# Attention inside one decoder step: the next head's projections placed between softmax steps, rope on VectorE, and the two softmax maps combined without dividing the first by its sum

## What is computed

```python
kv = rmsnorm(h, ln_kv) @ w_kv                      # K and V of all heads
k = rope(rmsnorm(k, k_norm), pos)                  # 2 maps of 64 channels each, 16 of 64 channels rotate
q = rope(rmsnorm((x @ w_q), q_norm), pos)
s = where(k_pos <= q_pos, q k^T / 8, min)          # for both maps m = 0, 1
p = softmax(s)
a = p[map 0] - lam * p[map 1]
o = a @ v                                          # sample tokens also over 256 cached positions
o = rmsnorm(o, subln) * (1 - lam_init)             # over the 128 value channels of a head
y = o @ w_out
```

## Time and profile before

| | us |
|---|---|
| Time, median of 3 runs | 3677.07 (3669.15 to 3680.99) |
| The profiled execution, its own time | 3693.18 |
| Its span, first to last instruction | 3691.4 |
| PE busy in it | 3396.5 (92%) |
| Attention, within the span | 1997 to 2801 |

### The profile page before, as it was taken

How to read it: one execution, slowest core, us unless ns; L and a number is a source line. 1 busy time by engine, 2 the same in 40 slices (tenths; PEclk the granted TensorE clock), 3 DMA queues, 4 the chain that set the end, 5 groups by cost and what they waited for, 6 DMA issues and landing times. The chain is left out here.

```text
span 3691.4 us, 60669 instructions
## 1 busy us (share of the span) xinstructions
PE 3396.5 (92%) x24063; PEld 3222.7 (87%) x24063; DVE 1512.6 (41%) x2316; ACT 1071.6 (29%) x1895; POOL 704.1 (19%) x453
## 2 busy tenths in 40 slices
PE   5898889988979999999999888888999999999998
PEld 5888878887869999999998777777878999999998
DVE  2554555455537222222234444444446422222223
ACT  2333343333321311111113344443343211111111
POOL 1212221222012311111113111111111321111110
PEclk7999999999969999999999899999999999999999
DMA  2010110011001111111111111111110111111111
GB/s 89 20 29 25 30 31 25 25 30 31 25 19 40 47 45 43 46 42 46 46 46 58 53 47 53 45 46 52 53 51 26 46 46 46 41 46 47 40 46 66
DMA packets 254695, 155.84 MB, mean 42 GB/s; under 512 B 9520, under 2 KB 251714, under 8 KB 254402
## 3 DMA queue, kind: packets, MB, share of 16 engines
q1 hardware_dynamic: 254426, 151.91, 14.1%
HBM read 133.46 MB, written 18.42 MB: 41 GB/s over the span
## 5 line engine op out<-in xcount | busy, mean ns | idle before, releaser
L212 PE MATMUL ps<-x_hi,w_hi 128*128 128x364 f32 x2808 | 667.2, 346 | 12.5 <-DVE w_lo L202 4.5
L212 PE MATMUL ps<-x_lo,w_hi 128*128 128x364 f32 x2808 | 621.8, 330 | 4.8 <-issue 4.8
L212 PE MATMUL ps<-x_hi,w_lo 128*128 128x364 f32 x2808 | 623.1, 330 | 0.0
L212 PEld LDWEIGHTS ps<-x_hi,w_hi 128*128 128x128 f32 x2808 | 486.4, 190 | 46.0 <-issue 11.5
L212 PEld LDWEIGHTS ps<-x_hi,w_lo 128*128 128x128 f32 x2808 | 491.0, 189 | 4.3 <-issue 4.3
L212 PEld LDWEIGHTS ps<-x_lo,w_hi 128*128 128x128 f32 x2808 | 490.2, 189 | 1.1 <-issue 1.1
L202 DVE TENSOR_TENSOR w_lo<-w_raw,w_hi 128x1024 fp32r<-128x1024 f32 x200 | 287.2, 1436 | 468.6 <-ACT w_hi L198 468.5
L198 ACT ACTIVATE w_hi<-w_raw 128x1024 fp32r<-128x1024 f32 x200 | 211.7, 1058 | 811.6 <-PE ps L212 594.1
L192 POOL TENSOR_TENSOR w_raw<-w_raw,params 128x1024 f32<-128x1024 f32 x120 | 234.0, 1950 | 928.8 <-DMA w_raw<-in_w_in_a 448.2
L1620 DVE TENSOR_TENSOR acc<-ps,acc 128x1092 f32<-128x1092 f32 x128 | 165.6, 1294 | 434.2 <-PE ps L212 434.2
L212 PE MATMUL ps<-hidden_hi,w_lo 128*128 128x364 f32 x1536 | 338.3, 328 | 0.0
(11 more groups left out here) (334 smaller groups left out, 4809.2 us busy)
## 6 DMA issues: line engine op xcount, KB each, us to landing
w_raw<-in_w_up SPq DMA_DIRECT2D x64, 512.0 KB, 3.9
w_raw<-in_w_down SPq DMA_DIRECT2D x64, 512.0 KB, 3.4
w_raw<-in_w_in_a SPq DMA_DIRECT2D x32, 512.0 KB, 4.2
w_raw<-in_w_kv SPq DMA_DIRECT2D x16, 512.0 KB, 4.0
cache_pages<-in_cache_k SPq DMA_DIRECT2D x128, 64.0 KB, 1.9
cache_pages<-in_cache_v SPq DMA_DIRECT2D x128, 64.0 KB, 1.9
x_in<-in_x_prompt SPq DMA_DIRECT2D x8, 512.0 KB, 4.2
state_sample<-in_state_delta SPq DMA_DIRECT2D x8, 512.0 KB, 4.0
```

The costliest lines, as they stand in the source:

```text
L212: mm = nc.tensor.matmul(PS[:, bank + g, 0:GRP], wt, x[:, k, g * GRP:(g + 1) * GRP], start=(k == 0 and t == 0), stop=(k == chunks - 1 and t ...
```

## The change

1. The slabs of a head are no longer a stage of their own. Those of head 0 are made ahead (`att_first_head_tensor`); those of head h+1 are made in nine units of 24 matmuls (one token group of one slab each, `unit_products`), placed by hand between the softmax steps of head h, with their evictions on DVE in groups of 364 columns. K and Q get a second pair of buffers; V goes through the last rows of MIX. The last head has only its softmax.
2. Rope: the permuting matmuls and POOL's four instructions go. SP copies the rotating rows from SBUF to SBUF (`swap`: four transfers of 8 partitions x 1088 elements for each of K and Q), and DVE does three instructions on 1088 columns for each (sine, cosine, add).
3. `combine` no longer scales map 0 by its reciprocal sum (L2215 goes). The row's factor would cancel in the following rms norm but for its eps; the eps term is carried by a second matmul in `out_sum`, whose weights are a broadcast column of squared sums, and whose result is added to the sum of squares.
4. SP reads the 16 page numbers once; the cached keys of the next head are fetched after the sample output of this one (now output 3, `SAMPLE_AT`, not 5), between the slab loads and swaps.
5. The third token group of every projection of the kernel is 360 columns wide, not 364.

```diff
+WIDTH = [GRP, GRP, T - 2 * GRP]
...
-                    mm = nc.tensor.matmul(PS[:, bank + g, 0:GRP], wt, x[:, k, g * GRP:(g + 1) * GRP],
+                    mm = nc.tensor.matmul(PS[:, bank + g, 0:WIDTH[g]], wt, x[:, k, g * GRP:g * GRP + WIDTH[g]],
                                           start=(k == 0 and t == 0), stop=(k == chunks - 1 and t == 2))
...
+        pages = [ds(sp.value_load(PGT[0:1, n:n + 1], min_val=0, max_val=cache_k.shape[0] - 1), 1)
+                 for n in range(NB * NPG)]
...
+        def key_pages(h, before=None):
+            head = ds(h, 1)
+            for n in range(NB * NPG):
+                src = cache_k[pages[n], :, head, :, :].rearrange("a t b m d -> (a t b) (m d)")
+                if n == 0 and before is not None:
+                    sp.wait_ge(b_pv.sem, b_pv.at(before, SAMPLE_AT + 1))
+                sp.dma_start(CP[:, n, :], src).then_inc(b_kin, 16)
+
+        def swap(a, i):
+            s = i[1]
+            i = 2 * i[0] + s
+            sp.wait_ge(b_nm.sem, b_nm.at(i))
+            for m in range(2):
+                one, two = (slice(m * B_HD + c * ROT // 2, m * B_HD + (c + 1) * ROT // 2) for c in range(2))
+                sp.dma_start(SWP[one, :], KS[a][s][two, 0:T]).then_inc(b_dx, 16)
+                sp.dma_start(SWP[two, :], KS[a][s][one, 0:T]).then_inc(b_dx, 16)
+
...
+        att_load(sp, 0, 0, 2)
+        key_pages(0)
+        att_load(sp, 0, 1, 0)
+        swap(0, (0, 0))
+        att_load(sp, 0, 1, 1)
+        swap(0, (0, 1))
+
...
+            if last:
+                return
+            if is_head(j, a, H - 2):
+                proj_b.load(sp, 0, 0)
+            else:
+                att_load(sp, j, a + 2, 0)
+            swap(1 - a, (h + 1, 0))
+            key_pages(h + 1, before=h)
+            if is_head(j, a, H - 2):
+                proj_b.load(sp, 0, 1)
+            else:
+                att_load(sp, j, a + 2, 1)
+            swap(1 - a, (h + 1, 1))
 
...
-    def kq_swaps(pe, s, i):
-        for c in range(3):
-            if c == 0:
-                pe.wait_ge(b_nm.sem, b_nm.at(i))
-            if c == 2:
-                pe.wait_ge(b_t1.sem, b_t1.at(i, 1))
-            nc.tensor.matmul(PS[:, 6 + c % 2, 0:GRP], SWAP[:, :], RB[s][:, c * GRP:(c + 1) * GRP],
-                             start=True, stop=True).then_inc(b_sw.sem, 1)
...
+    def unit_products(s, bank, g, ks):
+
+        for k in ks:
+            for t, (w, x) in enumerate(((WH, XH), (WH, XL), (WL, XH))):
+                mm = nc.tensor.matmul(PS[:, bank, 0:WIDTH[g]], w[s.slot][:, k, :], x[:, k, g * GRP:g * GRP + WIDTH[g]],
+                                      start=(k == 0 and t == 0), stop=(k == KC - 1 and t == 2))
+        return mm
+
+    def kq_sum(pe, h, s, g, bank):
+        i = 2 * h + s
+        pe.wait_ge(b_sq.sem, b_sq.at(i, g + 1))
+        nc.tensor.matmul(PS[:, bank, 0:GRP], BO64[:, :], SQB[:, (3 * s + g) % 2, :],
+                         start=True, stop=True).then_inc(b_pe.sem, 1)
 
...
     def out_sum(pe, h, p):
         pe.wait_ge(b_oc.sem, b_oc.at(h, 2 * p + 2))
-        if p > 0:
-            pe.wait_ge(b_on.sem, b_on.at(h, 2 * p - 1))
-        w = tile_width(out_tile(p))
-        nc.tensor.matmul(PS[:, 7, 0:w], ONES[:, :], SQO[p % 2][:, 0:w], start=True, stop=True).then_inc(b_os.sem, 1)
+        i = out_tile(p)
+        w = tile_width(i)
+        mm = nc.tensor.matmul(PS[:, 6, SUMS:SUMS + w], ONES[:, :], SQO[p % 2][:, 0:w], start=True, stop=i == NT)
+        if i < NT:
+            mm = nc.tensor.matmul(PS[:, 6, SUMS:SUMS + w], SC[:, i, 3, 0:1].to_broadcast([P, P]), IDENT[:, :],
+                                  start=False, stop=True)
+        mm.then_inc(b_os.sem, 1)
+
...
+            cache_keys(0)
+            cache_keys(1)
+            if not first:
+                out_sum(pe, h - 1, NT - 1)
+            pe.wait_ge(b_rp.sem, b_rp.at(2 * h))
+            if first:
+                pe.wait_ge(b_ev.sem, b_ev.at(0))
+            else:
+                pe.wait_ge(b_ex.sem, b_ex.at(h, 0))
+            for g in range(3):
+                for x in range(3):
+                    u = 3 * g + x
+                    w = tile_width(u)
+                    mm = nc.tensor.transpose(PS[0:w, g, x * P:(x + 1) * P], K[:, u * P:u * P + w], IDENT[:, :])
+                mm.then_inc(b_kt.sem, 1)
+            cache_keys(2)
+            cache_keys(3)
+            if not first:
+                values(pe, h - 1, NT)
...
+            k, q, v = (att_slab(j, a + 1, s) for s in range(3))
+
+            scores(pe, h, a, 1)
+            pe.wait_ge(w_lo.sem, w_lo.at(k.n))
+            unit_products(k, 7, 0, range(KC)).then_inc(b_un.sem, 1)
+            probs_transpose(pe, h, 0)
+            unit_products(k, 5, 1, range(KC)).then_inc(b_un.sem, 1)
+
+            scores(pe, h, a, 2)
+            pe.wait_ge(b_ev.sem, b_ev.at(h + 1, 1))
+            unit_products(k, 7, 2, range(KC)).then_inc(w_used.sem, 1)
+            probs_transpose(pe, h, 1)
+            pe.wait_ge(w_lo.sem, w_lo.at(q.n))
+            pe.wait_ge(b_ev.sem, b_ev.at(h + 1, 2))
+            unit_products(q, 5, 0, range(KC)).then_inc(b_un.sem, 1)
+            values(pe, h, 0)
+
+            scores(pe, h, a, 3)
+            out_sum(pe, h, 0)
+            pe.wait_ge(b_ev.sem, b_ev.at(h + 1, 3))
+            kq_sum(pe, h + 1, 0, 0, 7)
+            pe.wait_ge(b_ev.sem, b_ev.at(h + 1, 4))
+            unit_products(q, 5, 1, range(KC)).then_inc(b_un.sem, 1)
+            probs_transpose(pe, h, 2)
+            pe.wait_ge(b_ln.sem, b_ln.at(2 * h + 2, 1))
+            kq_sum(pe, h + 1, 0, 1, 7)
+            values(pe, h, 1)
+
+            scores(pe, h, a, 4)
+            out_sum(pe, h, 1)
+            pe.wait_ge(b_ln.sem, b_ln.at(2 * h + 2, 2))
+            kq_sum(pe, h + 1, 0, 2, 7)
+            pe.wait_ge(b_ev.sem, b_ev.at(h + 1, 5))
+            unit_products(q, 5, 2, range(0, 4))
+            probs_transpose(pe, h, 3)
+            unit_products(q, 5, 2, range(4, KC)).then_inc(w_used.sem, 1)
+            values(pe, h, 2)
+
+            scores(pe, h, a, 5)
+            out_sum(pe, h, 2)
+            pe.wait_ge(b_ln.sem, b_ln.at(2 * h + 2, 3))
+            kq_sum(pe, h + 1, 1, 0, 7)
+            values(pe, h, SAMPLE_AT)
+            pe.wait_ge(b_ev.sem, b_ev.at(h + 1, 6))
+            probs_transpose(pe, h, 4)
+            pe.wait_ge(b_ln.sem, b_ln.at(2 * h + 3, 1))
+            kq_sum(pe, h + 1, 1, 1, 7)
+            out_sum(pe, h, SAMPLE_AT)
+            values(pe, h, 4)
+
+            scores(pe, h, a, 6)
+            out_sum(pe, h, 4)
+            pe.wait_ge(b_ln.sem, b_ln.at(2 * h + 3, 2))
+            kq_sum(pe, h + 1, 1, 2, 7)
+            probs_transpose(pe, h, 5)
+            pe.wait_ge(w_lo.sem, w_lo.at(v.n))
+            pe.wait_ge(b_ln.sem, b_ln.at(2 * h + 3, 3))
+            unit_products(v, 7, 0, range(KC)).then_inc(b_un.sem, 1)
+            values(pe, h, 5)
+
+            scores(pe, h, a, 7)
+            out_sum(pe, h, 5)
+            pe.wait_ge(b_ev.sem, b_ev.at(h + 1, 7))
+            unit_products(v, 7, 1, range(0, 4))
+            probs_transpose(pe, h, 6)
+            unit_products(v, 7, 1, range(4, KC)).then_inc(b_un.sem, 1)
+            values(pe, h, 6)
+
+            out_sum(pe, h, 6)
+            pe.wait_ge(b_ev.sem, b_ev.at(h + 1, 8))
+            unit_products(v, 7, 2, range(0, 6))
+            probs_transpose(pe, h, 7)
+            unit_products(v, 7, 2, range(6, KC)).then_inc(w_used.sem, 1)
+            values(pe, h, 7)
 
...
+            n = 1 - a
+            exps(1)
+            hi_slab(act, att_slab(j, a + 1, 1))
+            probs_t(0)
+
+            exps(2)
+            att_square(act, n, h + 1, 0, 0)
+            probs_t(1)
+            att_square(act, n, h + 1, 0, 1)
+            att_out(act, h, 0)
+
+            att_out_rstd(act, h, 0)
+            att_ln(act, h + 1, 0, 0, 7)
+            exps(3)
+            att_square(act, n, h + 1, 0, 2)
+            probs_t(2)
+            att_ln(act, h + 1, 0, 1, 7)
+            att_out(act, h, 1)
+
+            att_out_rstd(act, h, 1)
+            att_ln(act, h + 1, 0, 2, 7)
+            exps(4)
+            att_rstd(act, h + 1, 0)
+            probs_t(3)
+            att_square(act, n, h + 1, 1, 0)
+            att_square(act, n, h + 1, 1, 1)
+            att_out(act, h, 2)
+
+            att_out_rstd(act, h, 2)
+            att_ln(act, h + 1, 1, 0, 7)
+            exps(5)
+            att_out(act, h, SAMPLE_AT)
+            att_square(act, n, h + 1, 1, 2)
+            probs_t(4)
+            att_ln(act, h + 1, 1, 1, 7)
+            att_out_rstd(act, h, SAMPLE_AT)
+            hi_slab(act, att_slab(j, a + 1, 2))
+            att_out(act, h, 4)
+
+            att_out_rstd(act, h, 4)
+            att_ln(act, h + 1, 1, 2, 7)
+            exps(6)
+            att_rstd(act, h + 1, 1)
+            probs_t(5)
+            att_out(act, h, 5)
+
+            att_out_rstd(act, h, 5)
+            exps(7)
+            probs_t(6)
+            att_out(act, h, 6)
+
```

(78 more changed lines are left out.)

509 lines of the change are left out of this document (269 added, 240 removed).

## The result

The changed kernel takes 3633.4 us (median of 4 runs, 3624.1 to 3641.7) where the kernel before takes 3679.0 beside it: ratio 0.9876, 95% interval 0.9837 to 0.9914. It is faster, as forecast, but by 46 us and not by 103, and its time lies above the range (3530 to 3620). The profiled execution took 3639.1 us, its span 3637.3.

What follows compares the result with a forecast made beforehand. PE, 92% busy, was taken as the bound. Interval 78.4 + 1.9 + 3.0 + 1.0 + 2.0 = 86.3 for 100.8 us; -101.5 + 6 - 2.5 - 5 = -103, applied to the 3677.1 median: 3574 us, range 3530 to 3620.

Steps and rivals of the forecast that it cites:

- Waits: PE's waits left in a head interval: 1.9 us in the sample stage, 3.0 for evictions and output copy, 1.0 short.
- the three waits that were to go: PE's softmax waits over seven intervals, for exponentials (32.6 us), combined probabilities (17.2) and output copy (11.2), go under filler.
- the V units' wait: Late softmax steps: PE waits about 2.3 us a head for an eviction before the last V unit, behind step 7's combine.
- Clock: Head intervals: half clock costs 2.0 us a head, between bounds 0 and 6.6, judged from PE's remaining idle time.
- PE's work: PE's work in one head at full clock: 80.6 us before, 78.4 after, with slab matmuls at 0.166 us.
- Head 0: Head 0's projections stay a stage; SP's page numbers and pages make PE late, once +6 us (0 to 10).
- Head 7: Last head, softmax alone: chain shorter by the dropped L2215, once -2.5 us.
- Widths: Projections outside the attention: 360 instead of 364 columns in the third group saves 5 us, at most 7.7.
- Swaps: SP's eight swap transfers a head, 0.33 us to issue and 1.9 to land each, cost nothing; slack 2.4 us.
- Rival C: Swaps land late, VectorE waits in steps 4 and 6; slower, 3764 us if landing takes 18 us; chance 0.04.
- Rival A: VectorE sets the last steps, held by GpSimd's three scalings: +4.9 us a head, interval 91.2, 3608 us; chance 0.20.
- Rival B: Head intervals: VectorE in time, clock stays at 1.00; interval 81.3 us, time 3539 us; chance 0.13.

Runs made afterwards that it cites:

- Experiments 4: Changed kernel with each sample-output page product multiplying all 64 columns of sample probabilities instead of its batch's 8, giving another sum; ratio 0.9811 to the kernel before.
- 7: Changed kernel with sample probabilities written block-diagonally into the zeroed sample-query buffer, so page products have 64 columns and the reference's output; ratio 0.9810 to the kernel before.
- run 8: Changed kernel with V unit 0 evicted ahead of step 7's maxima, head 0 reordered and 64-column block-diagonal sample probabilities; 3570.9 us, ratio 0.9680 to the kernel before.
- run 10: run 8 with the next head's first K unit moved from behind scores 1 into the sample softmax's wait; 3549.5 us, ratio 0.9644 to the kernel before.
- run 11: run 8 plus the changes of both run 10 and experiment 9; 3553.0 us, ratio 0.9668 to the kernel before.
- Experiment 12: Kernel before with only the block-diagonal sample probabilities, so sample-output page products have 64 columns; ratio 1.0002 to the kernel before.
- Experiment 3: Changed kernel with head 0's staging on SP and VectorE in another order, same work; ratio 0.9886 to the kernel before.
- experiment 9: run 8 with head 7 back in the order and bank of the kernel before; ratio 0.9704 to the kernel before.
- 5: Kernel before with only the undivided combination: L2215 gone, eps term as a second matmul in the output sums; ratio 0.9989 to the kernel before.
- experiment 1: Kernel before with only the third token group of every projection at 360 instead of 364 columns; ratio 1.0013 to the kernel before.
- experiment 6: Changed kernel with GpSimd scaling only one chunk in eight of each attention slab of heads 1 to 7; ratio 0.9852 to the kernel before.

## Why the prediction failed, step by step

**Waits: the sum right, one of them at another place.** Filler covers the chain; the three waits that were to go went, the sample `combine` kept its 11.3 us, and the V units' wait came, with the output copy's 3.6 us a head for 3.0; the short waits were 0.7 for 1.0, so the sum, 5.9, is the forecast's. That the numbers agree so well is in part luck. I had the V units wait 2.3 us for the eviction ahead of the last unit, behind the combine of step 7; no wait came there. PE waited ahead of the second unit, for the eviction of unit 0 behind the maxima of step 7: VectorE in order ahead of a V unit, as forecast, but at another place.

**Clock: the step that failed.** I took 2.0 us a head, arguing that PE's idle share falls to 5.9 of 86 us. It cost 5.2 (the interval's 91.3 less 80.2 of work, worked out below, and 5.9 of waits; 5.9 by half pace). I had taken idle time as the sign of what slows the clock. The rows ahead of the prediction showed 32 matmuls of 8 columns in 3.64 us, which I counted as full work; in the same trace 6.8 us at half clock begin at 2385.6, 1.4 us behind them. Experiments 4 and 7 show that with 64 columns instead of 8 the stretch behind them goes, two thirds of the half clock. The rest follows the two waits: with the V units' wait alone gone (run 8 beside 7) it doesn't shrink, with both gone (10, 11) it is 3.4 and 0 us. Experiment 12 shows that the half clock of before was no scale for its cost.

**PE's work, a little low.** 78.4 forecast. In run 11 no interval has any half clock, and PE is busy 561.36 of 573.70 us: 80.2 a head. So of the 5.0 us by which the interval was missed, 3.2 are the clock's and 1.8 the work's. The 0.166 us that I counted for a slab matmul was the MLP's; in units the 216 of a head took more, here in run 10:

```profile
2026.70:2601.70 575.00, 273.57 (x1512) 248.56 (x1512) 1.00 0.23 62
```

That is 39.1 us a head with the modelled tails of twelve blocks (three units are split in two). From one start to the next it is 0.173 us on average and 37.3 a head, for my 35.7. The projections of the kernel before, outside the slow stretches, took 0.174 in the same intervals, so it isn't the units' doing; why it is more than in the MLP no run here shows.

**Head 0: +20.1, not +6.** I had seen SP's order (page numbers ahead of the V slab, 16 pages ahead of K's swap) and not that of VectorE: the low part of Q's slab behind constants that wait for the page numbers' transfer (11.0 us), Q's evictions behind K's rope, V's behind Q's (9.2). Experiment 3 gave 18 of it back by order alone; it moved SP's and VectorE's instructions together, so their shares aren't told apart.

**Head 7: +8.1, not -2.5.** I had costed it by the dropped L2215 alone. In this head nothing lies between the steps, so each new wait of the values for the root of the last sum, and each sum behind the scores, is open; experiment 9 shows the order's share (2.5 to 4.7 us), and the narrow matmuls' lies between 1.1 and 4.8 us (59.5 to 63.2 us in the four profiles with 8 columns, 58.4 to 58.5 in the four with 64 and this order); 5 that the undivided combination gives 0.2 here.

**Widths: -5 forecast**, 6 to 7 by the starts of matmuls in the traces (an estimate, see experiment 1), below what the times can tell.

**Swaps: no cost in the intervals, right.** VectorE waits for them 3.6 and 3.4 us in head 0 alone; 16 key pages take 8.5 us to issue (9.5 forecast); a transfer of a swap takes 0.62 to 0.82 to issue where I took 0.33. Rival C is out. Rival A's time, 3608, was nearest of the four, and experiment 6 shows its cause nearly absent (0.9 us a head on VectorE for A's 4.9): that the interval came to 91.3 (A: 91.2) is luck. Rival B's 81.3 is nearly what run 10 reached, once the narrow matmuls and two waits were gone.

**What stays open:** what widths between 8 and 64 columns would do, which was not tried, why head 7's slow stretches differ by 5 us between runs 9 and 11, and why slab matmuls in the attention take 0.173 us from start to start where the MLP's take 0.166.

## What to carry to other kernels

Work placed between the steps of a latency chain pays as soon as it is longer than the chain, and then the order on the engine that frees the buffers is what is left: ask for each eviction what stands before it. Count a stretch of narrow matmuls as a risk to TensorE's clock even where PE shows no idle time, and look at the granted clock just behind it. Ask also whether PE is the bound there: less half clock gave time in the new order and none in run 12, where PE waits in each step. Cost a first and a last iteration by following every engine's list through it, not only the one that was changed.

## What the hardware showed unexpectedly

32 recorded matmuls of 8 columns, PE busy all the time, were followed by 6.8 or 10.2 us at 1.2 GHz in seven heads of seven; 32 of 64 columns took 3.8 us as well (start to end of the window above) and were followed by none. The Trainium skill (TensorE: Matmul & The Clock Gate, Part 1: The HAM clock gate) has the clock follow how busy PE has been; here PE's busy time in the trace was full either way, and the number of columns made the difference.

The collision of GpSimd's scaling with a VectorE instruction with two SBUF inputs is real (2.83 us for a combine of 896 columns that took 1.15 in six other heads), but it fell on such an instruction only four times in seven heads, and by experiment 6 it cost PE 0.4 us a head. The Trainium skill (SBUF — State Buffer, Who interferes with whom) has the collision; the trace agrees.

The delta stage, where nothing but the 360 columns changed, took 1082 to 1107 us in fourteen profiled executions, with 132 to 198 us of it at half clock: that alone moves the time of an execution by up to 0.7%, and an effect of a few us is to be read from its own stretch.
